# Ends of the attention stage reordered, and sliding attention's 64-row products made with 66 or 128 rows

## The reference, cut to what matters

```python
h = _rms_norm(x, norm_g) * (1 + scale) + shift
(qa, ka, va, fa, za, qb, kb, vb, zb, ga, gb) = split(h @ w_in)
# A: 8 heads of 64, causal, blocks of queries, logits + F_t - F_s
ya = (softmax(logitsA) @ va * silu(za)) @ w_o_fox
# B: 8 query heads, 2 key heads, keys of the own chunk of 64 and the one before
logits = einsum('bcqhgd,bcshd->bchgqs', qc, kb) * Dh ** -0.5 - slopes * dist
p = softmax(concatenate([logits, sink]))[..., :WK]
yb = (einsum('bchgqs,bcshd->bcqhgd', p, vb) * silu(zb)) @ w_o_swa
merged = sigmoid(ga) * ya + sigmoid(gb) * yb
x = x + gate * (merged @ w_out)
```

## Time and profile before

| | |
|---|---|
| runs | 2123.26, 2129.09, 2143.35 us; median 2129.09 |
| the profiled execution's own time | 2127.95 us |
| its span | 2126.2 us |
| granted clock of PE, mean | 0.962 |
| PE busy | 1979.7 us, 93% of the span |
| DVE, ACT, POOL busy | 885.6, 737.5, 550.5 us |
| attention stage | about 1105 to 1722 us |
| merge | to about 1936 us |

### The profile page before, as it was taken

One profiled execution on the slowest core, in us unless ns is written; L12 is line 12 of the kernel. 1 busy time (PEld: TensorE's weight loads), 2 busy tenths in 40 slices (PEclk: granted clock), 3 DMA queues, 4 the chain that ended last, 5 costly groups with the idle time before them and its releaser, 6 DMA issues. The chain is left out here.

```text
span 2126.2 us, 27983 instructions
## 1 busy us (share of the span) xinstructions
PE 1979.7 (93%) x9722; PEld 1555.5 (73%) x9722; DVE 885.6 (42%) x1851; ACT 737.5 (35%) x1375; POOL 550.5 (26%) x502
## 2 busy tenths in 40 slices
PE   7389999999999999999989899999999959998998
PEld 2368778798788788888866566666666639997887
DVE  2945555562212220000234455555565335554332
ACT  2622222220112132121115677767777751002000
POOL 1600000000000000000004576767777742110000
PEclk9589999999999999999986999999999979999999
DMA  6233443345512212121424446446464334232322
GB/s 238 98 101 89 120 119 99 118 133 136 134 50 89 78 49 89 49 89 58 124 74 95 96 112 159 113 92 144 108 141 99 74 122 137 80 99 99 119 91 77
DMA packets 235435, 222.63 MB, mean 105 GB/s; under 512 B 54610, under 2 KB 188498, under 8 KB 234292
## 3 DMA queue, kind: packets, MB, share of 16 engines
q1 hardware_dynamic: 221892, 180.95, 30.8%
q0 software_dynamic: 11648, 39.85, 5.9%
q10 hardware_dynamic: 1792, 0.53, 0.1%
HBM read 149.18 MB, written 71.70 MB: 104 GB/s over the span
## 5 line engine op out<-in xcount | busy, mean ns | idle before, releaser
L1242 POOL TENSOR_TENSOR Pl<-PT,Ph 128x512 fp32r<-128x512 f32 (+2 forms) x350 | 415.5, 1204 | 200.2 <-ACT Ph L1342 192.9
L474 PE MATMUL pj<-hTh,Wh 128*128 128x512 f32 x768 | 299.6, 390 | 0.7 <-DVE Wl L679 0.4
L475 PE MATMUL pj<-hTl,Wh 128*128 128x512 f32 x768 | 299.0, 389 | 0.0
L476 PE MATMUL pj<-hTh,Wl 128*128 128x512 f32 x768 | 298.9, 389 | 0.0
L474 PE MATMUL pj<-Wh,hTh 128*128 128x512 f32 (+1 forms) x640 | 246.1, 385 | 23.9 <-DVE Wl L679 23.9
L376 POOL DMA_DIRECT2D wraw<-in_w_in x84 | 45.1, 537 | 856.4 <-DVE Wl L679 850.3
L1335 ACT ACTIVATE PT<-sc 128x512 f32<-128x512 f32 (+2 forms) x350 | 192.6, 550 | 137.7 <-PE sc L1267 46.2
L476 PE MATMUL pj<-Wh,hTl 128*128 128x512 f32 (+1 forms) x640 | 240.0, 375 | 0.0
L475 PE MATMUL pj<-Wl,hTh 128*128 128x512 f32 (+1 forms) x640 | 239.9, 375 | 0.0
L1342 ACT ACTIVATE Ph<-PT 128x512 fp32r<-128x512 f32 (+2 forms) x350 | 207.9, 594 | 11.2
L1082 DVE TENSOR_REDUCE part_max<-mx 128x1 f32<-128x512 f32 (+3 forms) x267 | 157.6, 599 | 98.4 <-PE mx L1028 97.1
(11 more groups left out here) (231 smaller groups left out, 3553.5 us busy)
## 6 DMA issues: line engine op xcount, KB each, us to landing
qk_scratch<-qThl SPq DMA_DIRECT2D x96, 256.0 KB, 2.8
wraw<-in_w_in POOLq DMA_DIRECT2D x88, 256.0 KB, 3.8
g_scratch<-st SPq DMA_DIRECT2D x64, 256.0 KB, 2.4
gt<-g_scratch SPq DMA_DIRECT2D x16, 1024.0 KB, 7.8
xin<-in_x POOLq DMA_DIRECT2D x16, 512.0 KB, 5.0
wada<-in_w_ada SPq DMA_DIRECT2D x8, 1024.0 KB, 7.7
z_scratch<-st SPq DMA_DIRECT2D x32, 256.0 KB, 2.4
Qb<-qk_scratch SPq DMA_DIRECT2D x32, 256.0 KB
```

The lines of the kernel that those rows point to most:

```text
L474: nc.tensor.matmul(out, a_hi, b_hi, start=first, stop=False)
L475: nc.tensor.matmul(out, a_hi, b_lo, start=False, stop=False)
L476: return nc.tensor.matmul(out, a_lo, b_hi, start=False, stop=last)
L1242: pool.tensor_tensor(Pl[n % NPH][0:rows, 0:w], PT[n % NP][0:rows, 0:w], Ph[n % NPH][0:rows, 0:w].bitcast(F32), ALU.subtract).then_inc(low_ ...
```

## The change

**Rows.** The second product pair of a sliding row maximum reads 66 rows of QBa and KBa in place of 64: rows 64 and 65 of KBa are ones, those of QBa are zeros for the first two tiles, and later hold the shift of the tile before last in the same buffer, which DVE takes out again (one small DVE instruction more for each tile). The 64-row products of a step "B" use 128 rows, with zeros in the added rows of biasB and VB. DVE sets these zeros in its set-up.

**Start of attention.** No row maximum stands ahead of step 1; the bias tables are made from step 4 on; tile 0's row maxima stand at step 11; the first head holds its four sliding units in its last block, none in the third; the loads on SP are in another order.

**End of attention and start of merge.** The eighth group's inversion moves into the merge (`Finish`). The first four weight blocks are loaded during the last head. The first block of yh and yl is made in two halves, the first yl half by DVE.

The diff, cut to its core:

```diff
-        units = ((0, 1, 1, 2) if i >= JB else (0, 0, 1, 3))[j]
+        units = ((0, 1, 1, 2) if i >= JB else (0, 0, 0, 4))[j]
...
+    READY = 13
...
-    TABLES_AT, TABLE_TURNS = 1, 6
+    TABLES_AT, TABLE_TURNS = 4, 6
...
-            due = min(start - TILE_LEAD, due)
+            due = min(start - (TILE_LEAD if (kind, i) != ("s", 2) else 11), due)
             if (kind, i) == ("s", 0):
-                due = TABLES_AT + 7.5
+                due = TABLES_AT + 8.5
...
-    at = [None] * NU + [max(math.floor(due), START + u // 2) for u, (it, due) in enumerate(later)]
+    at = [None] * NU + [max(math.floor(due), 1 + u // 2) for u, (it, due) in enumerate(later)]
...
-    k_due = when(((h, c), START + 2 + 2 * c if h < 2 else last["f", (h - 2) * JB + 3] - AHEAD + 1 + 5 * c) for h in range(1, FOX_H) for c in range(JB))
-    q_due = when((i, START + i - NE + 1 if i < NQ else last["f", i - NQ] - AHEAD + 1) for i in range(NE, NB))
+    k_due = when(((h, c), START + 6 + c if h < 2 else last["f", (h - 2) * JB + 3] - AHEAD + 1 + 5 * c) for h in range(1, FOX_H) for c in range(JB))
+    q_due = when((i, START + 8 * (i - NE) if i < NQ else last["f", i - NQ] - AHEAD + 1) for i in range(NE, NB))
...
-    s_due = when((t, START + 1 + 7 * t if t < 2 else last["s", 2 * t - 3] + 1) for t in range(TT))
-    z_due = when((e, START + 2 + 2 * e if e < NZ else last[blocks[e - NZ]] + 2) for e in range(NBLK))
+    s_due = when((t, START + 4 + 11 * t if t < 2 else last["s", 2 * t - 3] + 1) for t in range(TT))
+    z_due = when((e, START + 1 + e if e < NZ else last[blocks[e - NZ]] + 2) for e in range(NBLK))
...
+    turns[-1] = NS + 1000
+    LAST = len(turns) - 1
...
-    TAIL = 28
+    TAIL = 2
...
-    biasA, biasB = sb("biasA", [P, SWA_H, P], F32R), sb("biasB", [HD, SWA_H, CHUNK], F32R)
+    biasA, biasB = sb("biasA", [P, SWA_H, P], F32R), sb("biasB", [P, SWA_H, CHUNK], F32R)
...
-    VB = [sb(f"VB{k}", [HD, KV_H, VW], F32R) for k in range(2)]
+    VB = [sb(f"VB{k}", [P, KV_H, VW], F32R) for k in range(2)]
...
+                    pe.wait_ge(ready, READY)
...
-                mm = nc.tensor.matmul(out[:, k, :], QBa[i % 2][0:HD, h0 + k, :], KBa[i % 2][0:HD, a, off:], start=False, stop=k == 1)
+                mm = nc.tensor.matmul(out[:, k, :], QBa[i % 2][0:HD + 2, h0 + k, :], KBa[i % 2][0:HD + 2, a, off:], start=False, stop=k == 1)
...
-                st.settle(nc.vector.scalar_tensor_tensor(shift[:, i % 2, 0], top[:, i % 2], -1.0, sinks_neg[:], ALU.mult, ALU.min))
+                st.settle(nc.vector.tensor_tensor(top[:, i % 2], shift[:, i % 2, 0], top[:, i % 2], ALU.subtract))
+                st.settle(nc.vector.tensor_tensor(shift[:, i % 2, 0], top[:, i % 2], sinks_neg[:], ALU.min))
...
+    def load_weights(sp):
+        sp.wait_ge(scored, last["f", (FOX_H - 1) * JB - 1] + 1)
+        for k, tile in enumerate(keep["early_rows"]):
+            sp.dma_start(tile, io["w_o_fox"][0, k * P:(k + 1) * P, :]).then_inc(keep["w_o_in"][k], 16)
+
+    class Finish:
+
+        def sums(self, sp):
+            load_sums(sp, LAST)
+
+        def inverses(self, sp):
+            store_inverses(sp, LAST)
+            load_inverses(sp, LAST)
+
+        def invert(self, dve):
+            invert(dve, LAST)
+
+        def scale(self, dve):
+            for m in range(4):
+                scale(dve, LAST, m)
+
+        def wait(self, eng):
+            eng.wait_ge(scaled, 4 * (LAST + 1))
...
-                    if n == START:
+                    if n == START + 1:
                         load_q(sp, NE - 1, (1,))
-                    if n == START + 1:
+                    if n == last["f", (FOX_H - 1) * JB - 1] + 2:
+                        load_weights(sp)
+                    if n == START + 3:
...
-                        mm = nc.tensor.matmul(out, identr[0:rows, 0:rows], (biasA if x == "A" else biasB)[:, heads, :], start=False, stop=True)
+                        mm = nc.tensor.matmul(out, identr[:, 0:rows], (biasA if x == "A" else biasB)[:, heads, :], start=False, stop=True)
...
-                                  by_head(Ph[n % NPH][0:rows, 0:w]), by_head(Pl[n % NPH][0:rows, 0:w]))]
+                                  by_head(Ph[n % NPH][:, 0:w]), by_head(Pl[n % NPH][:, 0:w]))]
...
+                        nc.vector.memset(QBa[k][HD:HD + 2, :, :].bitcast(F32), 0.0).then_inc(ready, 1)
+                        nc.vector.memset(VB[k][HD:P, :, :].bitcast(F32), 0.0).then_inc(ready, 1)
+                    nc.vector.memset(biasB[HD:P, :, :].bitcast(F32), 0.0).then_inc(ready, 1)
...
+                    st.settle(nc.vector.memset(shift[:], 0.0))
...
-        ring = [t[:] for t in keep["w_raw"]] + [spare[:, c:c + D] for c in range(0, 2 * KT * TB, D)]
-        load, high, low, w_split = split_rows(nc, ctx, "m", sources, ring, Wh, Wl)
+        ring = keep["early_rows"] + [spare[:, c:c + D] for c in range(2 * D, 2 * KT * TB, D)]
+        load, high, low, w_split = split_rows(nc, ctx, "m", sources, ring, Wh, Wl, keep["w_o_in"])
...
+            finish.sums(sp)
...
             load_gates(0, 0)
+            finish.inverses(sp)
             sp.wait_ge(w_split, KT)
             load_gates(0, 1)
...
+            low_y(0, 0, slice(BK, KT))
+            finish.wait(pool)
+            low_y(0, 1, slice(0, KT))
...
-            pe.wait_ge(y_split, 1)
             for k in range(KT):
                 pe.wait_ge(w_split, k + 1)
+                if k == BK:
+                    pe.wait_ge(y_split, 1)
...
+            high_y(0, 0, slice(0, BK))
+            high(act, 0)
+            high_y(0, 0, slice(BK, KT))
+            for k in range(1, KT):
...
+            dve.wait_ge(y_hi, 1)
+            nc.vector.tensor_tensor(yl[0][:, 0:BK, :], yT[:, 0:BK, 0:TB], yh[0][:, 0:BK, :].bitcast(F32), ALU.subtract)
             for k in range(KT):
                 low(dve, k)
-            with dve.Fori(0, NB // 2) as i:
+                if k == 1:
+                    finish.invert(dve)
...
+            gate(0, 0, range(BK))
+            finish.scale(dve)
+            gate(0, 0, range(BK, KT))
+            gate(0, 1)
```

140 lines of the change are left out of this document (79 added, 61 removed).

## The result

| | before | changed |
|---|---|---|
| runs, median (lowest to highest) | 2126.59 us (2123.26 to 2143.35) | 2104.42 us (2103.43 to 2108.51) |
| profiled execution, its span | 2127.95, 2126.2 us | 2105.39, 2103.7 us |
| granted clock, mean | 0.962 | 0.966 |
| PE busy | 1979.7 us | 1945.3 us |

The ratio is 0.9874, 95% interval 0.983 to 0.9919. The change gains 22 us as medians where 55 were forecast, and the time, 2104 us, lies 6 us above the upper end of the range. It lies 1 us from the 2103 us of the first rival (the pauses are not the rows'), but that is a coincidence of numbers: the pauses went, as the lines under part 1 show.

A forecast was written before the change was run, and what follows sets the result against it. PE was taken to set the pace; 27 + 13 + 15 = 55 us off the profiled 2127.95 us gives 2073 us, forecast as 2074 us since the runs' median is 1.1 us higher; range 2054 to 2098 us.

The forecast's parts named there:

- the first rival: 64-row pauses come from switching banks or operands, so the added rows give nothing: 2103 us, chance 10%.
- part 1: Attention after step 42: 66 or 128 rows in place of 64 remove PE's pauses, 27 us gained.
- part 2: Start of attention: the new order, with the rows' share there, gains 13 us, between 0 and 25.
- Early begin and bias tables, 3 + 3: Start of attention: PE begins earlier, 3 us gained; the wait for the last bias table goes, 3 us.
- Tile 2's load, 2.4: Start of attention: PE's wait for tile 2's VB shrinks from 6.2 to 3.8 us, 2.4 us gained.
- The new wait, -9: Start of attention: PE waits 5 to 7 us for tile 1's loads, half clock behind it, 9 us lost.
- The clock, 7: Start of attention: of about 12 us lost at half clock from 1131 to 1158.6 us, 7 return.
- Nine tenths: Share of the 30 us of pauses after step 42 taken to arrive, because of POOL: 27 us.
- 27 + 4.8: Gain from the added rows: 27 us after step 42, 4.8 us in the start of attention.
- the caution drawn from it, 5 us less: Sliding row maxima: the pause between the two 192-column products may stay, making the rows' sum about 5 us smaller.
- Part 3: Attention to merge: PE's first merge product comes 17 us earlier, less a 2 us wait, 15 us gained, 11 to 18.
- The wait in the merge's second block: Merge: PE waits for POOL's second yl, ready at 1757.5 us, needed at about 1756; 2 us, 0 to 5.

The follow-up runs named there:

- e2: Kernel before with only the new end of attention and start of merge: 2113.42 us, ratio 0.9925.
- e3: Changed kernel with the start order of before, new rows and new tail kept: 2089.84 us, ratio 0.9825.
- e14: Changed kernel with the zeros of QBa, VB and biasB set at step START + 8, behind DVE's first row maxima: 2100.21 us, ratio 0.9846.
- e9: e3 with DVE itself making the row copy (high part) that ACT made: 2085.49 us, ratio 0.9784.
- e8: e3 with a head's four K loads at every third step in place of every fifth: 2084.14 us, ratio 0.9783.
- e6: Changed kernel with tile 2's row maxima two steps earlier (lead 13 in place of 11): 2099.85 us, ratio 0.9859.
- e13: e3 with two edits of the new start: first head's sliding units in its last block, tile 2's lead 11 in place of 16: 2099.55 us, ratio 0.9844.
- e5: Changed kernel with tile 1's loads at an earlier step, ahead of the wait for block 1's output: 2098.14 us, ratio 0.9854.
- e11: Changed kernel with the edits of e5, e6 and e7 together: 2097.58 us, ratio 0.9851.
- e1: Kernel before with only the 66 and 128 rows, their zeros and DVE's extra instruction: 2106.09 us, ratio 0.9893.
- e10: e3 with both K loads at every third step and the row copy on DVE: 2066.63 us, ratio 0.971.
- e12: e10 with the 64-row products of before: 2096.3 us, ratio 0.9854.
- e7: Changed kernel with the five memsets of zeros moved from DVE's set-up to its step START + 4: 2103.94 us, ratio 0.9879.
- e15: e10 with causal row maxima not ahead of step 1, so PE begins with scores: 2068.56 us, ratio 0.9698.

## Why the prediction was wrong

**The failed step is part 2**, the start of attention, whose sum was 13 us. From the last product of `project` to step 67 the changed kernel needs 158.0 us, 3.0 more than before and 2.9 less than e2, not 13 less. The old start with the new rows takes 150.3 us there (e3). So the rows bring 4.6 us against before, where 4.8 were forecast, and 10.6 against e2; that the first agrees so well is luck of one execution. Of the 13 us the start itself was to gain 8, and it loses 7.6. By its terms:

- *Early begin and bias tables, 3 + 3*: PE begins 6.1 us sooner, pays 5.5 of it back at DVE's set-up, and step 10 stands 3.5 us sooner after `project` (32.9 against 36.4 us). e14 shows that the five memsets are worth 2.7 us there, half of the part_max wait. The bias wait fell from 3.2 to 0.6 us as forecast.
- *Tile 2's load, 2.4*: the wait is 3.7 us, 3.8 was forecast. Right.
- *The new wait, -9*: right in kind and place. The wait alone is 8.6 us where 5 to 7 were forecast, and the 5 us behind it run at half clock, so it cost about 11 by the same estimate. It wasn't the only one.
- *The clock, 7*: 54.6 us at half clock became 47.7. If at the half clock a microsecond loses half of one, an estimate, that is 3.5. And it wasn't the new start's doing: with the new rows and the old start there are 34 us at half clock in e3, 38 in e9 and 44 in e8 to step 67, no more than the 47.8 of the changed kernel.
- *What the sum lacked*: tile 2's shift rows on their way into QBa (3.1 us, in a stretch of 6.8 us at half clock), and a row copy (4.1 us, 1.05 before). The first comes from the lead of 11 steps in place of 16 for tile 2: two steps more leave 0.8 us (e6), and the old start with this lead and the new units has 4.7 us there (e13, which loses 2.6 us to step 67 by both edits). What makes the row copy late is open: it keeps 3.9 to 4.2 us in e5, e6 and e14, and e13's two edits alone leave it at 1.0. The prediction read the order on PE and SP for two places and asked nowhere else what each shortened lead had covered. It priced waits of the old order that go, and searched for only one that comes.

At step 42 the changed kernel and e3 are still level (110.2 and 110.4 us from `project`); the whole loss arises in steps 42 to 54, because the work moved there (94 products against 84 in the windows) isn't paid for by an earlier step 42, as it is in e13: the waits ahead have used that up. No single edit of the new start carries the loss: e5, e6, e14 and all three mends of e11 give back 1.4, 2.4, 1.7 and 4.6 of the 7.6 us. The profiles of e3 and the changed kernel differ by 10.5 us behind `project` (7.6 to step 67, 4.1 after it, -1.2 from step 349 on), and the 4.1 lie within the 451.2 to 457.8 us that the kernels with the same order there range over. They differ by another 5.3 us ahead of the end of `project`, where the code is the same; so of the two sizes for the start's cost, 15 us as medians and 10 by ratios, the profiles support the smaller.

**Part 1 was right in mechanism, wrong in the share that arrives.** The pauses measured as forecast, and the rival that they are not the rows' is refuted by the trace itself. "Nine tenths" of 30 us was the mis-sized step. As medians the rows give 18 to 24 us in the whole stage where 27 + 4.8 were forecast; in steps 67 to 349 alone 8.9 us arrive in the changed kernel, 11.3 in e1, 23.6 in e10. It looked at POOL's free quarter, and the waits on POOL did grow little (10.0 to 10.5 from step 67 on). It did not look at the K load and the row copy, whose 3.8 and 4.4 us of waits stood just below POOL's in the list of waits. A wait of a microsecond that occurs once a head is the sign of a lead used up: when the steps become shorter, part of what is gained in them is lost there. e8, e9, e10 and e12 show it: with the two leads mended the rows are worth 29.7 us of the 32 forecast in the whole stage.

The pause between the two equal 192-column products went too, 194 to 90 ns, so this trace shows one for each 64-row product. The Trainium skill (TensorEngine Tiling (Array Packing), Tiling Modes) says that changing the tiling mode, not just the tile, drains TensorE. That speaks of none between two products of the same mode, and the caution drawn from it, 5 us less, wasn't borne out. What a change of mode costs by itself no run here shows.

**Part 3 was right**: 14 us as medians (e2), 18.4 between the two profiles and 16.7 in that of e2, 15 forecast. PE's idleness before the merge is 4.95 us (5). The wait in the merge's second block came at 1752.12 with 2.3 us (2 forecast), at the end of POOL's yl (1751.69) as forecast; the trace names DVE's addition of 1747.75, which was stretched beside it to 4.22 us and ended 0.3 us later.

## What to carry to other kernels

When instructions of the pacing engine get shorter, list everything whose lead is counted in steps and whose wait isn't zero now, however small: those leads run out first, and behind such a wait there can be some microseconds at the half clock as well. An edit that moves many leads at once needs each shortened lead priced, and a stretch that grows is read together with the one ahead of it, from which work may have come. The version that keeps the rows and the tail, the old start, faster K loads and the row copy on DVE takes 2066.63 us, 38 less than the changed kernel (35 by ratios), and the last two of its four parts are one character and a few lines.

## What was not expected of the hardware

- The pause belongs to each 64-row product and vanishes at 66 rows: 194 to 90 ns between two alike, 271 to 180 into the first, 201 to 114 out of the last.
- An elementwise instruction of DVE can be stretched while POOL works. In the changed kernel an addition that takes 0.43 us took 4.22 and ended 0.3 us behind POOL's yl beside it; six more of these additions took 3.6 to 4.7 us, each with a yl beside it. In its set-up, with POOL at work on Pl, DVE shows

```profile
1112.90 0.67 DVE L1455 TENSOR_SCALAR R<-R 128x192 f32<-128x192 f32 x1
```

and in e7, where the same instruction came just ahead of POOL's first Pl (1105.85),

```profile
1105.48 0.26 DVE L1452 TENSOR_SCALAR R<-R 128x192 f32<-128x192 f32 x1
```

The set-up on which PE waited ended 15.5 us behind the last product of `project` in e3 and 17.9 in the changed kernel, with the same memsets; with the early begin alone added (e10 to e15) it went from 15.5 to 16.9. That POOL, which works sooner there, is the reason for all of it is argued from such pairs of lines and not tested. The prediction had the set-up end at 1116.2 us, 15.0 behind the last product of `project` in the trace of before, and no term for this.
- After the 3.42 us wait at 1457.18, PE, busy without a gap, ran 6.8 us at 1.2 GHz. A much shorter wait can have as much behind it: in e2 one of 1.2 us was followed by 10.2 us at that clock, one of 0.6 us by 3.4, and the kernel before, with the same products and waits of 1.15 us and less there, has 3.4 us in all where e2 has 20.5.
